# Attention projections of one decoder layer: the small matmul blocks between the weight chunks are gathered into one block per chunk

## The chip, the cores and the metric

One core of a Trainium2 chip runs the whole program. The metric is the device time of one execution in microseconds (us); for the kernel before it is the median of three runs. A profile of one further execution gives the trace. Five engines work side by side: PE (TensorE, matrix products), DVE (VectorE), ACT (ScalarE), POOL (GpSimd) and SP (SyncE, which here only issues transfers). PE reads SBUF and writes PSUM banks, which ACT and DVE empty.

## The reference, cut to what matters

One decoder layer is applied to 512 prompt rows and to 64 sample rows (8 sequences of 8 positions), with shared weights in float32:

```python
mod = silu(c) @ w_ada + b_ada          # 9 rows (1 prompt, 8 sample) x 6144, split in six
h = rmsnorm(x) * (1 + scale) + shift   # 512 + 64 rows of 1024
z = h @ w_in                           # q, k, v of three head groups, then u, v, gates
A = dilated attention per group        # group 0: window 128; 1: stride 4; 2: stride 16
B = spatial gating of u and v
x = x + gate1 * ((sig(gA) * A @ w_pa + sig(gB) * B @ w_pb) @ w_o)
x = x + gate2 * two-level mixture of experts(norm(x))
y = rmsnorm(x) modulated by silu(c) @ w_ada_final + b_ada_final
```

The keys and values of the sample rows' past come from three caches.

## The kernel before

**Weights come through a ring.** SP loads a list of pieces (`stream`, filled by `put`, `put_chunks` and `put_ada`) into four slots of 2 MB, in the list's order; piece n goes to slot n % 4 once piece n - 4 has been read (`wait_slot_read`). A weight chunk is 1024 x 512, loaded as two halves of 1 MB (k = 0 to 3 and 4 to 7). A half fills the front of its slot raw; ACT writes its rounded high part behind it (`split_to`, L1575), and DVE overwrites the raw values with the low part, raw minus high (L1891). The products of the 512 prompt rows use high and low parts in three passes: `three_passes`, L997 to L999, per tile of 128 rows and half 4 x 3 matmuls of 512 columns; `half_product` does one such tile.

**Sample rows.** Their product with a chunk is made from the raw values (`samples_product`, L1039: 16 matmul records of 256 columns for a half, in two 64-column parts of the array). So DVE may write the low part of a half only after PE has read its raw values: it waits in `wait_samples_read`.

**Modulation steps.** The rows `mod` that are needed later (G = 1 to 3, 2048 columns each) are computed between the attention projections, in eight steps k of one PSUM bank each (`ada_step`, L1012: 8 matmul records of 512 columns, in four 32-column parts of the array). A step needs 1 MB of weights, which is one piece of the ring, in a slot of its own.

**Order on PE.** For g = 0, 1, 2 there are three chunks q, k and w (w holds the v values). `project` runs half 0 on four tiles, then half 1 on four tiles. Inside a half, before tile `at_[half]`, it puts the sample product of one half: in half 0 that of the chunk's own second half, in half 1 that of the next chunk's first half. After each half comes one modulation step:

```python
                    if ada_from is not None:
                        ada_step(g + 1, ada_from + half)
```

So a k chunk has four small blocks: sample rows, step, sample rows, step. After w come transposes of q and k (L985), scores (L1174), exponentials on ACT (L1660), and values (`tile_values`, transposes at L985 and L1196), with steps 6 and 7 between the scores. For g < 2 the chunk q of the next group is computed before the values of the fourth tile; its first sample half comes before the values of the third. The ring's order is that of use: half, step, half, step for each chunk, then steps 6 and 7; after group 2 come the cached keys and values (SP issues from L726). `store_rows` sends finished modulation rows to DRAM, issued by SP five pieces behind a group's last step.

DVE empties k (L2077), ACT empties q and w (L1564); the list of PSUM users fixes the order.

Of the kernel before, what the change touches and what calls it, by code (L numbers as in the profile page):

```python
# [14 lines left out]
P = 128  # L15
D = 1024
KD = D // P
# [204 lines left out]
def build(nc, t, out):  # L222

    ctx = ExitStack()
    with ctx:
# [48 lines left out]
        def slot(n):  # L274
            return at((n % SLOTS) * SLOT, SLOT)
# [268 lines left out]
        ADA_COLS = 4 * CH  # L544
# [8 lines left out]
        def put(name, last, *srcs):  # L553
            S0.setdefault(name, []).extend(range(len(stream), len(stream) + len(srcs)))
            stream.extend(srcs)
            slot_last.extend(last)
            split.extend([False] * len(srcs))

        def put_chunks(name, last, w, js, between=None):

            for j, pair_ in zip(js, last):
                for m, h in zip(pair_, halves(w, j)):
                    put(name, [m], h)
                    split[-1] = True
                    if between is not None:
                        put_ada(between, 1)

        def paired(name, j):

# [20 lines left out]

            return [(mm.bank(m)[64 * q:64 * q + NS, 256 * q:256 * q + 256], slice(256 * q, 256 * q + 256)) for q in range(2)]

        def put_ada(G, count):
            w, _, col = ada[G]
            for _ in range(count):
                k = len(S0.get(f"ada{G}", []))
                put(f"ada{G}", [("ada", KD * G + k)],
                    w[k * P:(k + 1) * P, col * ADA_COLS:(col + 1) * ADA_COLS].unsqueeze(1))

        put_ada(0, KD)  # L600
        put_chunks("v", projected("v", 2), w_in, [QKV // CH + 2 + j for j in range(2)])
# [3 lines left out]
        for g in range(3):  # L605
            for j, x in enumerate("qkw"):
                put_chunks(f"{x}{g}", projected(f"{x}{g}"), w_in, [3 * j + g], between=g + 1)
            put_ada(g + 1, 2)
        caches = [t[f"cache_kv_w{w}"][0] for w in WINS]

        def keys_of(b, kv, g):
# [362 lines left out]
        def _(pe):  # L974
# [28 lines left out]

            def ada_step(G, k):

                n = S0[f"ada{G}"][k]
                slot_wait(n)
                if k == 0 and G:
                    pe.wait_ge(ada_out, G)
                w = slot(n)[:, 0:ADA_COLS].rearrange("p (j n) -> p j n", j=4)  # L1010
                for j in range(4):
                    ins = nc.tensor.matmul(ada_bank[32 * j:32 * j + 32, :], cT[:, k, :], w[:, j, :],  # L1012
                                           start=(k == 0), stop=(k == KD - 1))
                ins.then_inc(ada_read, 1)

            def project(name, lhs, j, g=0, ada_from=None, ahead=(None, None), at_=(1, 1), between=None):

                for half in range(2):
                    tiles = range(4) if paired(name, j) else range(TILES)
                    for i in tiles:  # L1020
                        if i == at_[half] and ahead[half] is not None:
                            samples_product(*ahead[half], 1 - half)
                        half_product(name, lhs, j, g, half, i)
                        if between is not None:
                            between(half, i)
                    if ada_from is not None:
                        ada_step(g + 1, ada_from + half)

            def samples_product(name, j, lhs, half):

# [166 lines left out]
                                               vn[:, kt, h * DH:(h + 1) * DH], start=(kk == 0), stop=(kk == nk - 1))  # L1197
                ins.then_inc(mm_filled, 1)

            def ahead_of(x, y):  # L1200

                return ((x, 0, h4_raw), (y, 0, h4_raw) if y else None)

            project("q0", H_PARTS, 0, ada_from=0, ahead=ahead_of("q0", "k0"), at_=(3, 3))
            for g in range(3):
                project(f"k{g}", H_PARTS, 0, g=g, ada_from=2, ahead=ahead_of(f"k{g}", f"w{g}"), at_=(3, 3))
                project(f"w{g}", H_PARTS, 0, g=g, ada_from=4, ahead=ahead_of(f"w{g}", None), at_=(3, 3))
                for j, src in enumerate((qn, kn)):

                    mm.wait_emptied(pe, mm.first[f"{'qk'[j]}{g}"] + TILES - 1)  # L1210
                    for i in range(TILES):
                        transposes(tp.first[f"qk{g}"], TILES * j + i, ROWS[i],
                                   [src[0:ROWS[i], i, k * P:(k + 1) * P] for k in range(4)])
                tp.wait_emptied(pe, tp.first[f"qk{g}"] + 2 * TILES - 1)
                tiles = GT[4 * g:4 * g + 4]
                tile_scores(*tiles[0])
                tile_scores(*tiles[1])
                ada_step(g + 1, 6)
                ada_step(g + 1, 7)
                tile_scores(*tiles[2])  # L1220
                tile_values(*tiles[0])
                tile_scores(*tiles[3])
                tile_values(*tiles[1])
                if g < 2:
                    samples_product(f"q{g + 1}", 0, h4_raw, 0)
                tile_values(*tiles[2])
                if g < 2:
                    project(f"q{g + 1}", H_PARTS, 0, g=g + 1, ada_from=0, ahead=ahead_of(f"q{g + 1}", f"k{g + 1}"),
                            at_=(1, 3))
                tile_values(*tiles[3])  # L1230


            def key_tile(b, x):
# [638 lines left out]
        def _(dve):  # L1872
# [11 lines left out]
            def split_to(last):  # L1884

                for n in range(parted[0], min(last + 1, N_SLOTS)):
                    if split[n]:
                        raw, hi, lo = half_slot(n)
                        dve.wait_ge(hi_done, halves_to[n])
                        wait_samples_read(dve, n)  # L1890
                        V.tensor_tensor(lo, raw, hi, ALU.subtract).then_inc(lo_done, 1)  # L1891
                    parted[0] = n + 1
# [173 lines left out]
            for g in range(3):  # L2066
                split_to(S0[f"k{g}"][1])
                if g:
                    dve.wait_ge(kv_out, 16 * KV_OUTS[g - 1])
                for i in tile_order(f"k{g}", 0):  # L2070
                    n = ROWS[i]
                    m = bank_of(f"k{g}", 0, i)
                    if i == 3:
                        split_to(S0[f"w{g}"][0])
                    mm.wait_filled(dve, m)
                    for src, cols in quarters(m) if i == 4 else [(mm.bank(m), slice(0, CH))]:
                        ins = V.tensor_copy(kn[0:n, i, cols], src)  # L2077
                    ins.then_inc(mm_dve, 1)
                split_to(S0[f"w{g}"][1])
                dve.wait_ge(abias_in, 16 * (g + 2))  # L2080
                add_bias(*GT[4 * g])
                add_bias(*GT[4 * g + 1])
                ada_rows(g + 1)
                for i in (2, 3):
                    add_bias(*GT[4 * g + i])
                    copy_out(g, i - 2)
                if g < 2:
                    split_to(S0[f"q{g + 1}"][0])
                copy_out(g, 2)
                if g < 2:  # L2090
                    split_to(S0[f"k{g + 1}"][0])
                copy_out(g, 3)

            def group_differences():
# [412 lines left out]
```

## Time and profile before

| | |
|---|---|
| median of 3 runs | 1317.78 us (1312.26 to 1319.25) |
| the profiled execution | 1314.65 us |
| its span, first to last instruction | 1313.0 us |
| PE busy | 1237.6 us, 94% of the span |
| DVE, ACT, POOL busy | 50%, 42%, 15% |
| mean granted clock of PE | 0.982 of full speed |
| transfers | 293.96 MB, mean 224 GB/s |

The span is 1.65 us shorter than the time of that execution. The stretch in which the change lies runs from about 264 to 603 us of the span. Matmul durations overlap each other, so the cost of a block is read from the start of its first matmul to the start of what follows.

### The profile page before, as it was taken

Reading aid. Unit: us, or ns where it says so; the run is one execution under the profiler, and the core shown is the slowest. Engines: PE = TensorE matmul, PEld = TensorE weight load, DVE = VectorE, ACT = ScalarE, POOL = GpSimd, SP = SyncE. Lnnn points to the kernel's source line nnn. Section 1 sums busy time; section 2 is a strip of 40 time slices with the busy share of each in tenths; the row PEclk is TensorE's granted clock in tenths of the full one; section 3 lists DMA queues with packets and bytes.
Section 4 is the critical chain, followed back from the end, with each engine's and each line's share of the span. In section 5 each row is a group of like instructions: output and inputs, shape, how many; then the busy total and the mean of one; then the engine's idle time right before and its main releaser. Section 6 shows DMA issues by size and latency. Waiting matters only on the chain.

```text
span 1313.0 us, 17979 instructions
## 1 busy us (share of the span) xinstructions
PE 1237.6 (94%) x7160; PEld 941.9 (72%) x7160; DVE 661.7 (50%) x920; ACT 548.7 (42%) x878; POOL 194.0 (15%) x228
## 2 busy tenths in 40 slices
PE   4899999999999999999889999999989999999996
PEld 1677877776778887887756666747757887777762
DVE  1328513222161205032377551255687888888877
ACT  3623313002272126214433332211446787777852
POOL 1202200020000010001200010100034122222320
PEclk9899999999999999999799999999989999999999
DMA  9552221154443454537689995911399999999982
GB/s 357 209 209 76 94 64 64 65 190 173 152 146 85 159 178 176 171 128 275 238 295 382 384 374 172 304 64 53 104 318 296 371 374 374 372 373 378 366 301 91
DMA packets 126235, 293.96 MB, mean 224 GB/s; under 512 B 10160, under 2 KB 10288, under 8 KB 121496
## 3 DMA queue, kind: packets, MB, share of 16 engines
q1 hardware_dynamic: 108216, 243.57, 52.7%
q0 software_dynamic: 17952, 49.44, 10.5%
q8 instruction: 49, 0.80, 0.2%
q14 instruction: 18, 0.15, 0.0%
HBM read 269.91 MB, written 30.42 MB: 229 GB/s over the span
## 4 chain that ended last, share of the span: by engine, by line
PE 78%; DMA 11%; DVE 4%; ACT 4%; issue 2%; POOL 2%; SPq 0%; DVEq 0%; ACTq 0%; POOLq 0%
PE psum L997 18%; PE psum L999 17%; PE psum L998 17%; PE psum L985 5%; PE psum L1039 5%; DMA arena<-in_cache_kv_w_dram 3%; DMA arena<-in_w_gate_dram 2%; PE psum L1360 2%; PE psum L1196 2%; PE psum L1012 2%; DMA arena<-in_w_ada_dram 2%; PE psum L1268 2%; ACT arena L1564 1%; POOL slots_d L915 1%; PE psum L1174 1%
## 5 line engine op out<-in xcount | busy, mean ns | idle before, releaser
L997 PE MATMUL psum<-part,part 128*128 128x512 f32 (+1 forms) x1088 | 442.4, 407 | 10.6 <-DVE part L1942 5.0
L999 PE MATMUL psum<-part,part 128*128 128x512 f32 (+1 forms) x1088 | 429.4, 395 | 0.0
L998 PE MATMUL psum<-part,part 128*128 128x512 f32 (+1 forms) x1088 | 429.3, 395 | 0.0
L997 PEld LDWEIGHTS psum<-part,part 128*128 128x128 f32 (+1 forms) x1088 | 227.4, 209 | 74.3 <-issue 24.8
L999 PEld LDWEIGHTS psum<-part,part 128*128 128x128 f32 (+1 forms) x1088 | 227.3, 209 | 40.1
L998 PEld LDWEIGHTS psum<-part,part 128*128 128x128 f32 (+1 forms) x1088 | 228.1, 210 | 35.7
L2360 DVE TENSOR_TENSOR part<-arena,part 128x2048 fp32r<-128x2048 f32 x96 | 218.9, 2291 | 33.5 <-ACT part L1792 32.3
L1891 DVE TENSOR_TENSOR part<-arena,part 128x2048 fp32r<-128x2048 f32 x42 | 96.4, 2301 | 254.5 <-PE psum L1039 228.7
L1792 ACT ACTIVATE part<-arena 128x2048 fp32r<-128x2048 f32 x94 | 179.7, 1919 | 45.1 <-DMA arena<-in_w_down_dram 19.5
L1564 ACT ACTIVATE arena<-psum 128x512 f32<-128x512 f32 (+3 forms) x140 | 75.9, 567 | 248.4 <-PE psum L999 202.7
L1575 ACT ACTIVATE part<-arena 128x2048 fp32r<-128x2048 f32 x42 | 80.0, 1910 | 173.2 <-DMA arena<-in_w_in_dram 168.6
L985 PE MATMUL psum<-cst,arena 128*128 128x128 f32 (+2 forms) x858 | 117.7, 282 | 26.9 <-DMA cst<-in_consts_dram 12.4
L985 PEld LDWEIGHTS psum<-cst,arena 128*128 128x128 f32 (+2 forms) x858 | 96.2, 146 | 57.0 <-issue 15.9
L1039 PE MATMUL psum<-arena 128*64 128x256 f32 x544 | 66.0, 385 | 0.2 <-DMA arena<-in_w_in_dram 0.2
L169 ACT ACTIVATE arena<-psum 128x512 f32<-128x512 f32 x56 | 33.4, 596 | 57.7 <-PE psum L985 57.6
L2043 DVE TENSOR_TENSOR arena<-psum,arena 128x512 f32<-128x512 f32 x30 | 19.0, 684 | 75.1 <-PE psum L1174 66.4
L1039 PEld LDWEIGHTS psum<-arena 128*64 128x64 f32 x544 | 36.1, 136 | 25.6 <-issue 9.1
L950 POOL DMA_INDIRECT yd<-arena x15 | 32.4, 2161 | 98.3 <-issue 91.5
L1268 PE MATMUL psum<-arena 128*32 128x136 f32 (+1 forms) x832 | 37.8, 284 | 9.1 <-ACT arena L169 5.9
L171 DVE COPY arena<-psum 128x512 f32<-128x512 f32 x48 | 33.0, 687 | 21.6 <-PE psum L985 21.2
L1660 ACT ACTIVATE arena<-arena 128x128 f32<-128x128 f32 (+1 forms) x96 | 39.6, 419 | 6.9 <-DVE arena L2049 6.9
L1012 PE MATMUL psum<-arena 128*32 128x512 f32 x256 | 35.8, 642 | 6.3 <-DMA arena<-in_w_ada_dram 6.3
(289 smaller groups left out, 1071.2 us busy)
## 6 DMA issues: line engine op xcount, KB each, us to landing
arena<-in_w_in_dram SPq DMA_DIRECT2D x34, 1024.0 KB, 5.5
arena<-in_cache_kv_w_dram SPq DMA_DIRECT2D x16, 2048.0 KB, 11.9
arena<-in_w_gate_dram SPq DMA_DIRECT2D x32, 1024.0 KB, 9.9
arena<-in_w_up_dram SPq DMA_DIRECT2D x32, 1024.0 KB, 9.4
arena<-in_w_down_dram SPq DMA_DIRECT2D x32, 1024.0 KB, 10.2
arena<-in_w_ada_dram SPq DMA_DIRECT2D x24, 1024.0 KB, 7.7
arena<-in_cache_kv_w_dram SPq DMA_DIRECT2D x16, 1024.0 KB, 9.0
arena<-in_w_ada_final_dram SPq DMA_DIRECT2D x8, 1024.0 KB, 7.9
```

What stands on the lines that cost most here:

```text
L985: ins = nc.tensor.transpose(bank[0:a.shape[-1], k * n:k * n + a.shape[0]], a, c_("ident", a.shape[0])[:, 0:a.shape[0]])
L997: nc.tensor.matmul(out_, hi, w_hi, start=start, stop=False)
L998: nc.tensor.matmul(out_, hi, w_lo, start=False, stop=False)
L999: last_product[0] = nc.tensor.matmul(out_, lo, w_hi, start=False, stop=stop)
L1012: ins = nc.tensor.matmul(ada_bank[32 * j:32 * j + 32, :], cT[:, k, :], w[:, j, :], start=(k == 0), stop=(k == KD - 1))
L1039: ins = nc.tensor.matmul(out_, lhs[:, 4 * half + k, :], raw[:, k, cols], start=(half == 0 and k == 0), stop=(half == 1 and k == 3))
L1268: ins = nc.tensor.matmul(mm.bank(m)[r, cols], Qm[:, b % 2 * 2048 + quad * 512 + j * P:b % 2 * 2048 + quad * 512 + (j + 1) * P][:, r], KT[: ...
L1564: nc.scalar.activation(dst, ring.bank(m)[0:n, 0:cols] if src is None else src, func, scale=scale).then_inc(ring.done(m), 1)
L1575: nc.scalar.activation(hi, raw, ACT.Copy).then_inc(hi_done, 1)
L1792: nc.scalar.activation(hi, raw, ACT.Copy).then_inc(e_hi, 1)
L1891: V.tensor_tensor(lo, raw, hi, ALU.subtract).then_inc(lo_done, 1)
L2360: V.tensor_tensor(lo, raw, hi, ALU.subtract).then_inc(e_lo, 1)
```

## The change

The two modulation steps that followed the two halves of a chunk become one piece of the ring: 256 rows x 2048 columns, 2 MB, the two rows of a partition side by side in one slot. Steps 6 and 7 also share a piece. `ada_at` says where a step is found. The 42 pieces of the three groups become 30.

On PE, `project` of a k or w chunk has nothing between its tiles. A new `between_chunks` runs between chunks: both sample halves of the next chunk, then two modulation steps. After w there are the two steps alone. The q chunks keep the sample product of their own second half inside half 0 (before the second tile; for q0 it was before the fourth). For q1 and q2 the block that prepares k stands behind the values of the fourth tile. DVE makes the low part of k's first half after it has copied out those values, where it was before.

```diff
@@ -562,8 +562,8 @@
                     put(name, [m], h)
                     split[-1] = True
-                    if between is not None:
-                        put_ada(between, 1)
+                if between is not None:
+                    put_ada(between, 2, 2)
...
-        def put_ada(G, count):
+        ada_at = [[] for _ in ada]
+
+        def put_ada(G, count, together=1):
+
             w, _, col = ada[G]
-            for _ in range(count):
-                k = len(S0.get(f"ada{G}", []))
-                put(f"ada{G}", [("ada", KD * G + k)],
-                    w[k * P:(k + 1) * P, col * ADA_COLS:(col + 1) * ADA_COLS].unsqueeze(1))
+            for _ in range(count // together):
+                k = len(ada_at[G])
+                rows = w[k * P:(k + together) * P, col * ADA_COLS:(col + 1) * ADA_COLS]
+                ada_at[G] += [(len(stream), c) for c in range(together)]
+                put(f"ada{G}", [("ada", KD * G + k + together - 1)], rows.rearrange("(k p) n -> p k n", p=P))
...
-            put_ada(g + 1, 2)
+            put_ada(g + 1, 2, 2)
...
-                    if ada_from is not None:
-                        ada_step(g + 1, ada_from + half)
+
+            def between_chunks(following, G, k):
+
+                if following is not None:
+                    for half in range(2):
+                        samples_product(following, 0, h4_raw, half)
+                for step in range(2):
+                    ada_step(G, k + step)
...
-            project("q0", H_PARTS, 0, ada_from=0, ahead=ahead_of("q0", "k0"), at_=(3, 3))
+            project("q0", H_PARTS, 0, ahead=(("q0", 0, h4_raw), None))
+            between_chunks("k0", 1, 0)
             for g in range(3):
-                project(f"k{g}", H_PARTS, 0, g=g, ada_from=2, ahead=ahead_of(f"k{g}", f"w{g}"), at_=(3, 3))
-                project(f"w{g}", H_PARTS, 0, g=g, ada_from=4, ahead=ahead_of(f"w{g}", None), at_=(3, 3))
+                project(f"k{g}", H_PARTS, 0, g=g)
+                between_chunks(f"w{g}", g + 1, 2)
+                project(f"w{g}", H_PARTS, 0, g=g)
+                between_chunks(None, g + 1, 4)
...
-                    project(f"q{g + 1}", H_PARTS, 0, g=g + 1, ada_from=0, ahead=ahead_of(f"q{g + 1}", f"k{g + 1}"),
-                            at_=(1, 3))
+                    project(f"q{g + 1}", H_PARTS, 0, g=g + 1, ahead=((f"q{g + 1}", 0, h4_raw), None))
                 tile_values(*tiles[3])
+                if g < 2:
+                    between_chunks(f"k{g + 1}", g + 2, 0)
...
                 if g < 2:
-                    split_to(S0[f"k{g + 1}"][0])
+                    split_to(S0[f"q{g + 1}"][1])
                 copy_out(g, 3)
```

## Rows read from the trace of the kernel before

**Rows 1.** The page: PE's share of the chain that ended last.
```profile
PE 78%; DMA 11%; DVE 4%; ACT 4%; issue 2%; POOL 2%; SPq 0%; DVEq 0%; ACTq 0%; POOLq 0%
```

**Rows 2.** Busy time by stretch: PE, PEld, DVE, ACT, POOL, clock, DMA share, GB/s.
```profile
283.00:365.00 82.00, 80.32 (x422) 56.81 (x421) 14.99 (x11) 18.91 (x27) 2.15 (x4) 1.00 0.47 167
...
645.00:825.00 180.00, 168.54 (x1728) 118.92 (x1727) 99.23 (x299) 65.08 (x188) 22.05 (x38) 0.98 0.92 324
```

**Rows 3.** Lines L1039 and L1012 on PE, 274 to 645 us: records, nanoseconds.
```profile
L1039 PE MATMUL psum<-arena x272: 379/379/431, 283.1 to 587.2; 128*64 128x256 f32 x136
...
L1012 PE MATMUL psum<-arena x192: 592/593/617, 287.9 to 615.2; 128*32 128x512 f32 x192
```

**Rows 4.** Timeline of PE: a sample block between two products of group 0.
```profile
297.01 0.39 PE L999 MATMUL psum<-part,part 128*128 128x512 f32 x1
297.32 1.95 PE L1039 MATMUL psum<-arena 128*64 128x256 f32 x16
299.20 0.50 PE L997 MATMUL psum<-part,part 128*128 128x512 f32 x1
299.54 0.40 PE L998 MATMUL psum<-part,part 128*128 128x512 f32 x1
```

**Rows 5.** Timeline of PE in q1: a modulation step between two products.
```profile
407.43 0.39 PE L998 MATMUL psum<-part,part 128*128 128x512 f32 x1
407.66 0.40 PE L999 MATMUL psum<-part,part 128*128 128x512 f32 x1
407.99 1.06 PE L1012 MATMUL psum<-arena 128*32 128x512 f32 x8
408.99 0.62 PE L997 MATMUL psum<-part,part 128*128 128x512 f32 x1
409.45 0.40 PE L998 MATMUL psum<-part,part 128*128 128x512 f32 x1
```

**Rows 6.** Timeline of PE: two sample halves, and two steps, without a gap.
```profile
819.85 3.67 PE L1039 MATMUL psum<-arena 128*64 128x256 f32 x32
823.45 1.06 PE L1314 MATMUL psum<-cst,arena 128*128 128x8 f32 x8
...
368.85 1.92 PE L1012 MATMUL psum<-arena 128*32 128x512 f32 x16
370.70 2.82 PE L1174 MATMUL psum<-arena 64*128 64x128 f32 x32
```

**Rows 7.** Timeline of PE: 32-column work, then a sample block.
```profile
784.14 2.78 PE L1306 MATMUL psum<-arena 128*32 128x512 f32 x24
786.85 1.95 PE L1039 MATMUL psum<-arena 128*64 128x256 f32 x16
```

**Rows 8.** Timeline of PE at the end of q1.
```profile
422.79 1.06 PE L1012 MATMUL psum<-arena 128*32 128x512 f32 x8
423.79 1.09 PE L985 MATMUL psum<-cst,arena 128*128 128x128 f32 x8
```

**Rows 9.** Timeline of ACT at the end of q1.
```profile
422.90 0.60 ACT L1564 ACTIVATE arena<-psum 128x512 f32<-128x512 f32 x1 [2.65 <-PE psum L999]
```

**Rows 10.** Timeline of PE, and the chain: the sample block that w0's load holds up.
```profile
325.42 0.39 PE L999 MATMUL psum<-part,part 128*128 128x512 f32 x1
326.00 1.95 PE L1039 MATMUL psum<-arena 128*64 128x256 f32 x16 [0.19 <-DMA arena<-in_w_in_dram]
...
320.40 5.55 DMA arena<-in_w_in_dram
```

**Rows 11.** Timeline of DVE: the low part of k0's first half.
```profile
299.39 2.29 DVE L1891 TENSOR_TENSOR part<-arena,part 128x2048 fp32r<-128x2048 f32 x1 [11.91 <-PE psum L1039]
```

**Rows 12.** Transfers issued at L726, 590 to 700 us: PE's waits for them.
```profile
  PEld psum L985: 0.4, 1
  PE psum L985: 0.2, 1
```

**Rows 13.** Busy time at the end of group 2, columns as in rows 2.
```profile
626.00:641.00 15.00, 13.33 (x63) 12.41 (x63) 3.58 (x6) 8.36 (x35) 2.16 (x4) 0.54 0.43 159
```

**Rows 14.** Timeline of PE in that stretch.
```profile
628.13 1.97 PE L985 MATMUL psum<-cst,arena 128*128 128x128 f32 x8 [1.49 <-ACT arena L1660]
```

More of the change, by code:

```diff
@@ L1004, in ada_step @@
             def ada_step(G, k):
-                n = S0[f"ada{G}"][k]
+                n, c = ada_at[G][k]
                 slot_wait(n)
@@ L1009, in ada_step @@
                     pe.wait_ge(ada_out, G)
-                w = slot(n)[:, 0:ADA_COLS].rearrange("p (j n) -> p j n", j=4)
+                w = slot(n)[:, c * ADA_COLS:(c + 1) * ADA_COLS].rearrange("p (j n) -> p j n", j=4)
                 for j in range(4):
@@ L1014, in ada_step, with project @@
                 ins.then_inc(ada_read, 1)
-            def project(name, lhs, j, g=0, ada_from=None, ahead=(None, None), at_=(1, 1), between=None):
+            def project(name, lhs, j, g=0, ahead=(None, None), at_=(1, 1), between=None):
                 for half in range(2):
@@ L1198, in tile_values @@
                 ins.then_inc(mm_filled, 1)
-            def ahead_of(x, y):
-                return ((x, 0, h4_raw), (y, 0, h4_raw) if y else None)
-            project("q0", H_PARTS, 0, ada_from=0, ahead=ahead_of("q0", "k0"), at_=(3, 3))
+            project("q0", H_PARTS, 0, ahead=(("q0", 0, h4_raw), None), at_=(3, 3))
+            between_chunks("k0", 1, 0)
             for g in range(3):
-                project(f"k{g}", H_PARTS, 0, g=g, ada_from=2, ahead=ahead_of(f"k{g}", f"w{g}"), at_=(3, 3))
-                project(f"w{g}", H_PARTS, 0, g=g, ada_from=4, ahead=ahead_of(f"w{g}", None), at_=(3, 3))
+                project(f"k{g}", H_PARTS, 0, g=g)
+                between_chunks(f"w{g}", g + 1, 2)
+                project(f"w{g}", H_PARTS, 0, g=g)
+                between_chunks(None, g + 1, 4)
                 for j, src in enumerate((qn, kn)):
```

## The prediction

> **What bounds the kernel now.** I read the page first, for the chain that ended last: PE carries 78% of it [rows 1]. So time taken out of PE's own sequence counts, if what follows is not bound by something else. Next the busy time by stretch. In the attention projections PE is busy 80.3 of 82 us at full clock with transfers at 0.47 of their capacity; in the stage of the cached keys that follows, transfers are at 0.92 [rows 2]. The change lies in the first kind of stretch, and what it saves must pass through the second. Third, the lines: 272 records of sample products are 17 blocks of 16, and 192 of modulation steps are 24 steps of 8, all between 283 and 616 us [rows 3]. The change keeps every one of them; it alters only what stands beside them. So I went to the timeline of PE and measured edges, from start to start.
>
> **What an edge costs.** A modulation step in q1: products start 0.23 us apart, the step starts 0.33 us after the last product, it occupies 1.00 us until the next product starts, and the second product comes 0.46 us behind the first, where the pace is 0.23 [rows 5]. The edge in and out is 0.10 + 0.22 = 0.32 us. In group 0, where the prompt rows are contiguous and not taken with stride 4, the same two gaps are 0.31 and 0.34, so 0.08 + 0.11, about 0.20 us for both, and the sample half occupies 1.88 us [rows 4]. Two sample halves that follow each other take 3.60 us until the next work starts, not 3.76, and two steps take 1.85 us, not 2.00 [rows 6]. So each block ends with about 0.15 us in which the array empties, and a neighbour of the same kind saves that.
>
> **Group 0.** Between products there were ten blocks: q0's own second half, step, k0's first half, step; in k0 four; in w0 two. One more step stands at the end of w0. Now there are three (q0's sample half, and one block before k0 and one before w0). Seven edges less are 7 x 0.20 = 1.40 us. Five pairs of equals have come together (sample with sample twice, step with step three times, the end of w0 included): 5 x 0.155 = 0.78 us. Sum 2.2 us.
>
> **A wait that goes.** The sample product for w0 starts 0.58 us after the product before it, where others take 0.31: w0's first half, issued at 320.40, took 5.55 us to land [rows 10]. It was waiting for the slot of k0's first half, two tiles before use. In the new order it takes the slot of the modulation piece read before k0, a whole chunk ahead. 0.26 us off, once; the other such blocks don't wait.
>
> **Groups 1 and 2.** Nine blocks stood between products (q three, k four, w two); two remain (q's own second half, the block before w). 7 x 0.32 = 2.24 us. The five pairs give 0.78 again. The step at the end of q goes from there: it took 1.00 us up to the transposes [rows 8], and is counted in a pair. The block that takes it in stands behind the values instead, where products began anyway with their slow first gap. For this new boundary I charge one emptying, 0.15 us, bounded by 0 and by the 0.32 of a full edge. Sum 2.87 us for each group, 5.7 for both.
>
> **Inside the new block** there is one meeting of unlike kinds: 64-column sample products, then 32-column steps. No row shows that order. The reverse order does: 24 matmuls of 32 columns take 2.71 us until the sample block starts [rows 7], which is 24 x 0.107 (half of a step's pace of 0.85 for 8, from rows 6) plus 0.15, a full emptying. I take it as not saved. If it were free, six blocks would give 6 x 0.15 = 0.9 us more. The Trainium skill, "TensorEngine Tiling (Array Packing)", section Key Properties, says that changing the tiling mode, not just the tile, drains TensorE; by it the meeting costs the emptying, as I took it. The rows at hand agree, with the 0.15 us of rows 7, but it also appears where like follows like with another output.
>
> **What could be late now.** (a) The low part of k's first half. DVE started it 2.07 us after the sample block's start and needs 2.29 us [rows 11]; that block began at 297.32 [rows 4]: ready after 4.4 us. The first product comes 3.60 + 1.85 = 5.45 us after the block's start: 1.1 us of slack, covered by the second sample half and the steps. DVE's copy of the values, now ahead of it, ends before the raw half is read. Without that cover each of six blocks would lose up to 4.4 us less what still stood in between. (b) The second half of the next chunk must be in when its raw product starts. Its slot is free after the first tile of the running chunk's second half. From rows 10, the issue would be at 320.40; three tiles of 12 products at 0.23 (2.75 us each), the edge and one sample half of 1.7 us put its use some 10.0 us later. The load took 5.55 us there: 4.4 us of slack. (c) The 2 MB modulation piece is issued when a chunk ends and used a chunk (22 us) later. SP's other issues are not moved past anything that PE needs: the row stores still stand five pieces behind the last step, behind a piece that waits for the same chunk q, and the pieces number 12 fewer, a multiple of four, so every later piece keeps its slot. (d) ACT: at the end of q1 it emptied the last tile from 422.90 to 423.50, under cover of the step [rows 9]. With the transposes 1.0 us earlier, their first tile would be ready at about 423.4, so ACT is late by 0.1 us at most, twice. DVE now copies k's last tile after w's low part, 5 us into the block; its bank is asked for three tiles into w. Nothing.
>
> **Sum.** 2.2 + 0.3 + 5.7 - 0.1 = 8.1 us, with bounds of 7.4 (the new boundary at 0.32, ACT late by 0.2 each time) and 9.3 (both free). The profiled execution took 1314.65 us, 3.1 under the median of 1317.78; from it the change gives 1306.5, from the median 1309.7. The three runs and the profiled one average 1316.0. I say 1308. What a measurement of this kernel can tell from no change is 0.5%, 6.6 us; 8.1 us is 0.62%, just over.
>
> **Rivals.**
> (1) The saving is partly absorbed. The key stage runs on transfers at 0.92. If the transfers were already the limit when group 2 ends, PE would only wait longer. For: the share. Against: PE's waits for these transfers from 590 to 700 us are 0.4 and 0.2 us [rows 12], and the cached pieces are issued as the ring's slots come free, which moves with PE. Gains in group 2 alone (2.9 us) would be at risk first, then all. I put it at a gain of 2 to 5 us: 1311 to 1315. Chance 0.13.
> (2) The clock. At the end of group 2 PE waits 1.49 us for exponentials and then works at about half clock: eight transposes take 1.97 us, not 1.09 [rows 8, 14], granted clock 0.54 over 15 us [rows 13]. That costs up to 13.3 x 0.46 = 6.1 us. The same waits come 8 us earlier. If the fall comes at another point of that sequence, the gain may grow to 12 us or shrink to 3. The rows can't say which. Also, longer unbroken runs of products change nothing where the clock is already 1.00 [rows 2]. 1303 to 1306 with chance 0.08, 1311 to 1314 with 0.09.
> (3) Slower: the second half lands late. Place: all six new blocks, where PE stands at the raw product with everything behind it. The price is the landing time less 10.0 us. It would eat the whole gain at 8.1 / 6 = 1.35 us each, so at landings of 11.4 us; slower by 0.5% at 2.45 us each, landings of 12.5 us, which gives 1325. Transfers do take that long in crowded stretches. Against: 5.55 us in just this place [rows 10] and a DMA share of 0.47, and nothing else is queued ahead on SP. Chance 0.07.
> (4) The edges shrink the forecast: the emptying belongs to what follows and is paid once per block whatever precedes, so only edges go and the pairs give nothing: 1.4 + 2 x 2.1 + 0.3 = 5.9 us, 1310 from my base, within 0.5%. Against it, rows 6. Chance 0.06.
> The forecast itself: 0.57.
>
> **How the numbers follow.** Faster by over 0.5%: of the forecast's 0.57 I count 0.50 (7.4 to 9.3 us is over 6.6, and some of it is lost to the measurement's spread), the clock's good side 0.08, and 0.04 of the rest: 0.62. Slower by over 0.5%: rival 3 and little else, 0.08. Within: 0.30. The range: the forecast's own, 1305 to 1311, is widened by the runs' spread of 7 us (1312.26 to 1319.25) to about 1302 to 1314. It takes in the good side of the clock at the low end and the absorbed gain up to the old median at the high end: 1301 to 1317. What is left out is the late landing and the far tails.
>
> **What the profile after would show.** Two runs of 96 products without a break in k and w of each group; before them 32 records of L1039 and 16 of L1012 that take 5.4 to 5.5 us to the next product. The steps 6 and 7 of the first group should end about 2.5 us earlier than at 370.7 [rows 6], and the last matmul of a step should start about 8 us earlier than at 615.2 [rows 3]. Waits of PE for DVE's low part or for w_in near zero. From 660 us on, everything earlier by one constant. Wrong would be: a first product that waits for DVE behind a block (a), a gap in the middle of L1039's 32 records (b), or an interval from the last step to the first key scores that has grown (rival 1 or 2).

## The result, and the profile after

The new kernel takes 1311.21 us (median of 19 runs, 1306.88 to 1317.64) against 1319.25 us (19 runs, 1312.26 to 1323.95): ratio 0.9944, 95% interval 0.9928 to 0.9961. The ratio makes it 7.4 us less, 5.1 to 9.5 by the interval; the two medians are 8.0 apart. The forecast was 8.1 us, and a time of 1308.

One thing was misread ahead of the prediction. The new line for q0 is `project("q0", H_PARTS, 0, ahead=(("q0", 0, h4_raw), None), at_=(3, 3))`: q0's sample block stays before the fourth tile, as in the kernel before, and is not moved to the second. No term of the sum used it.

**The blocks on PE.** The new line numbers are 4 to 10 higher: L1001 to L1003 are the three passes, L1049 the sample products, L1016 the modulation steps, L989 the transposes. The timeline of PE in the profiled execution of the new kernel, at the boundary from q0 to k0, at the end of q1, and at the start of k1:

```profile
298.15 0.39 PE L1003 MATMUL psum<-part,part 128*128 128x512 f32 x1
298.47 3.67 PE L1049 MATMUL psum<-arena 128*64 128x256 f32 x32
302.07 1.92 PE L1016 MATMUL psum<-arena 128*32 128x512 f32 x16
303.93 0.50 PE L1001 MATMUL psum<-part,part 128*128 128x512 f32 x1
304.26 0.39 PE L1002 MATMUL psum<-part,part 128*128 128x512 f32 x1
...
416.03 0.40 PE L1003 MATMUL psum<-part,part 128*128 128x512 f32 x1
416.27 0.49 PE L989 MATMUL psum<-cst,arena 128*128 128x128 f32 x3
...
422.72 3.67 PE L1049 MATMUL psum<-arena 128*64 128x256 f32 x32
426.33 1.92 PE L1016 MATMUL psum<-arena 128*32 128x512 f32 x16
428.18 0.63 PE L1001 MATMUL psum<-part,part 128*128 128x512 f32 x1
```

From start to start: 3.60 us for two sample halves, 1.86 for two steps, and the same edges as in [rows 4]. The meeting of the sample products with the steps saves nothing: the samples take 3.60 us to the next start here, as before other work in [rows 6]. The end of q1 holds what the prediction missed: transposes right behind products start 0.24 us after the last one, at the pace of the products. The step that stood there before started 0.33 us behind them, an entry edge of 0.10 that is gone as well.

A sample half that products on 64 columns follow, in the gate chunk of the new kernel:

```profile
185.57 1.95 PE L1049 MATMUL psum<-arena 128*64 128x256 f32 x16
187.45 0.44 PE L1001 MATMUL psum<-part,part 128*64 128x512 f32 x1
```

It takes 1.88 us up to them, as it does up to products on the full array.

**The waits.** All waits of PE between 262 and 600 us of the new kernel (line, who released it; sum, times, longest):

```profile
PE psum L989 <- ACT arena L1574: 3.1, 13, 0.3
PE psum L1206 <- ACT arena L1574: 2.6, 8, 0.4
PE psum L1184 <- ACT arena L1574: 0.9, 2, 0.5
PE psum L989 <- ACT arena L1670: 0.8, 1, 0.8
```

None is for DVE's low part, none for a transfer. The wait of [rows 10] is gone. DVE still starts 2.06 us after the block, and the loads of the chunk halves land as fast as before; first the timeline of DVE, then the time from issue to landing of the 16 issues of w_in between 262 and 600 us:

```profile
300.53 4.50 DVE L1901 TENSOR_TENSOR part<-arena,part 128x2048 fp32r<-128x2048 f32 x2 [13.41 <-PE psum L1049]
```

```profile
DMA to landing us min/median/max: 5.2/5.4/7.8
```

The longest, 7.8 us, is below the 10.0 that the second half has.

**Where the gain stands along the way.** I count from the start of the sample block near 264 us, a block that both kernels have just ahead of the change, to the first transpose behind w2. In the kernel before 264.50 to 604.26, so 339.76 us; in the new one 264.15 to 595.50, so 331.35 us: 8.41 us less. Group by group it is 2.56, 2.93 and 2.92.

Behind that point the sequence is that of the kernel before. The busy time of the stretch that answers to [rows 13], in the new kernel (PE, PEld, DVE, ACT, POOL, clock, DMA share, GB/s):

```profile
617.00:632.00 15.00, 13.33 (x64) 12.41 (x64) 3.47 (x5) 8.46 (x36) 2.05 (x4) 0.58 0.15 52
645.00:825.00 180.00, 166.94 (x1625) 117.01 (x1626) 95.92 (x290) 62.04 (x180) 21.05 (x37) 0.98 0.91 323
```

The clock falls at the same work, with the same 1.49 us of wait in front of it. The span of the profiled execution is only 4.8 us shorter as a whole (1308.2 against 1313.0). PE's share of the chain that ended last went from 78% [rows 1] to 73%; the page of the new kernel:

```profile
span 1308.2 us, 17967 instructions
...
PE 73%; DMA 14%; ACT 4%; DVE 4%; issue 3%; POOL 2%; SPq 0%; DVEq 0%; ACTq 0%; POOLq 0%
```

The chain now passes through more transfers of w_gate in the experts (5% of the span, before 2%), some 500 us behind the change. Whether that belongs to the change is a question for the experiments.

### The profile page after: what moved, and what is told of

Same layout as the page of the kernel before. It is cut to its first block, busy times and chain, and to the rows that moved or that the text cites. A ratio compares the mean times of both kernels' runs of the same rounds, so it can differ in the third digit from the quotient of the medians.

```text
span 1308.2 us, 17967 instructions
## 1 busy us (share of the span) xinstructions
PE 1231.0 (94%) x7160; PEld 941.8 (72%) x7160; DVE 660.4 (50%) x920; ACT 547.9 (42%) x878; POOL 194.9 (15%) x228
## 4 chain that ended last, share of the span: by engine, by line
PE 73%; DMA 14%; ACT 4%; DVE 4%; issue 3%; POOL 2%; SPq 0%; DVEq 0%; ACTq 0%; POOLq 0%
PE psum L1001 17%; PE psum L1003 16%; PE psum L1002 16%; DMA arena<-in_w_gate_dram 5%; PE psum L989 5%; PE psum L1049 5%; DMA arena<-in_cache_kv_w_dram 3%; PE psum L1370 2%; PE psum L1206 2%; PE psum L1016 2%; ACT arena L1574 2%; DMA arena<-in_w_ada_dram 2%; DMA arena<-in_w_in_dram 1%; PE psum L1278 1%; POOL slots_d L919 1%
## 5 line engine op out<-in xcount | busy, mean ns | idle before, releaser
L1001 PE MATMUL psum<-part,part 128*128 128x512 f32 (+1 forms) x1088 | 439.0, 404 | 11.4 <-DVE part L1952 5.9
L1003 PE MATMUL psum<-part,part 128*128 128x512 f32 (+1 forms) x1088 | 429.6, 395 | 0.0
L1001 PEld LDWEIGHTS psum<-part,part 128*128 128x128 f32 (+1 forms) x1088 | 227.6, 209 | 66.2 <-issue 13.4
L1003 PEld LDWEIGHTS psum<-part,part 128*128 128x128 f32 (+1 forms) x1088 | 227.5, 209 | 40.1
L989 PE MATMUL psum<-cst,arena 128*128 128x128 f32 (+2 forms) x858 | 117.0, 281 | 25.8 <-DMA cst<-in_consts_dram 11.7
L989 PEld LDWEIGHTS psum<-cst,arena 128*128 128x128 f32 (+2 forms) x858 | 95.2, 145 | 55.4 <-issue 17.6
L1049 PE MATMUL psum<-arena 128*64 128x256 f32 x544 | 64.7, 384 | 0.2 <-DMA arena<-in_w_in_dram 0.2
L1049 PEld LDWEIGHTS psum<-arena 128*64 128x64 f32 x544 | 36.6, 136 | 24.5 <-issue 8.2
L1278 PEld LDWEIGHTS psum<-arena 128*32 128x32 f32 (+1 forms) x832 | 29.3, 117 | 15.9 <-issue 13.5
```

The costliest lines, as they stand in the source:

```text
L989: ins = nc.tensor.transpose(bank[0:a.shape[-1], k * n:k * n + a.shape[0]], a, c_("ident", a.shape[0])[:, 0:a.shape[0]])
L1001: nc.tensor.matmul(out_, hi, w_hi, start=start, stop=False)
L1003: last_product[0] = nc.tensor.matmul(out_, lo, w_hi, start=False, stop=stop)
L1049: ins = nc.tensor.matmul(out_, lhs[:, 4 * half + k, :], raw[:, k, cols], start=(half == 0 and k == 0), stop=(half == 1 and k == 3))
L1278: ins = nc.tensor.matmul(mm.bank(m)[r, cols], Qm[:, b % 2 * 2048 + quad * 512 + j * P:b % 2 * 2048 + quad * 512 + (j + 1) * P][:, r], KT[: ...
```

## The experiments

The theory to test: the gain is PE time at the edges of small blocks, plus the emptying that neighbours of one kind share; the pairing of the pieces only makes the gathering possible; the order inside the block hides DVE. The rivals: larger transfers help by themselves; the order inside doesn't matter; a part of the gain is lost to the transfers of the later stages.

Times stand as ratios to the kernel before, with intervals. The distance is that from the sample block near 264 us to the first transpose after w2, read from the starts on PE.

| kernel | distance, us | against the new one | ratio |
|---|---|---|---|
| before, three profiles | 339.76, 339.92, 340.09 | +8.4 to +8.7 | 1 |
| new, four profiles | 331.35, 331.37, 331.35, 331.35 | 0 | 0.9944, again 0.9941 |
| old order, paired pieces | 339.54 | +8.19 | 1.0 (0.9981 to 1.0019) |
| new order, single pieces | 367.69 | +36.3 | 1.0165 (1.0126 to 1.0203) |
| only the steps gathered | 338.18 | +6.83 | 0.9983 (0.9962 to 1.0004) |
| only the samples gathered | 333.97 | +2.62 | 0.9947 (0.9928 to 0.9965) |
| steps first in the block | 336.21 | +4.86 | 0.997 (0.9954 to 0.9986) |
| carried further | 331.01 | -0.34 | 0.993 (0.9912 to 0.9948) |

The distance repeats to 0.02 us over four profiles of the new kernel and to 0.33 over three of the kernel before, so it tells apart what times of 1300 us with a spread of 10 can't. The other kernels have one profile each.

### The pieces alone, with the old order

```diff
-            between_chunks("k0", 1, 0)
+            project("q0", H_PARTS, 0, ada_from=0, ahead=ahead_of("q0", "k0"), at_=(3, 3))
...
+                    if ada_from is not None and half in step_after:
+                        ada_step(g + 1, ada_from + step_after.index(half))
```

> PE does its blocks in the order of the kernel before; only the ring's pieces are those of the new kernel (two steps in one 2 MB piece, 30 pieces and not 42). Theory (the gain is the edges beside the small blocks): nothing but the wait for w0's first half goes, 0.3 us; the transposes after w2 start within 0.5 us of the kernel before, reckoned from the first sample block at 264 us, and the ratio to it is 1.000. Rival (fewer and larger transfers are what helps): several us faster, ratio near 0.995.

The distance is 0.22 us shorter than in the first profile of the kernel before and 0.55 shorter than in the third, the wait of [rows 10] and little more, and the ratio is 1.0. PE waits for no transfer of w_in in this stretch. Fewer and larger transfers bring nothing by themselves.

### The new order, each step in a piece of its own

```diff
-                    put_ada(between, 2, 2)
+                    put_ada(between, 2)
...
-            put_ada(g + 1, 2, 2)
+            put_ada(g + 1, 2)
```

> PE does its blocks in the order of the new kernel, but each modulation step keeps a piece and a slot of its own. Theory (the pairing's work is to free a slot, so that the next chunk's second half is in when its sample product is gathered): that half now waits for the slot of the running chunk's second half, so it is issued at the chunk's end and lands 5.5 us later, 3.9 us too late, before k0 and before w0, w1 and w2; before k1 and k2 the values cover most of it. Some 16 us of waits of PE for w_in, time about 1326, ratio to the kernel before about 1.006. Rival (pieces don't matter, only the order on PE): the same as the new kernel, ratio 0.994.

The time is 1342.09 us (4 runs), 16 us more than the theory gave. The timeline of PE between q0 and k0, then busy time and clock there and in k0:

```profile
298.58 1.95 PE L1049 MATMUL psum<-arena 128*64 128x256 f32 x16
303.95 3.68 PE L1049 MATMUL psum<-arena 128*64 128x256 f32 x16 [3.42 <-DMA arena<-in_w_in_dram]
307.56 2.83 PE L1016 MATMUL psum<-arena 128*32 128x512 f32 x16
310.32 0.50 PE L1001 MATMUL psum<-part,part 128*128 128x512 f32 x1
```

```profile
298.00:312.00 14.00, 10.58 (x58) 4.95 (x58) 5.34 (x4) 3.00 (x4) 0.00 (x0) 0.76 0.32 99
312.00:332.00 20.00, 20.00 (x89) 16.52 (x88) 2.07 (x3) 1.92 (x1) 0.00 (x0) 1.00 0.38 141
```

The wait itself is as forecast: 3.42 us here, 16.7 us over five blocks, where the theory had about 16.

```profile
PE psum L1049 <- DMA arena<-in_w_in_dram: 16.7, 5, 3.6
```

What it left out is what comes behind a wait. The second sample half took 3.61 us and not 1.88, the steps 2.76 and not 1.85, at a granted clock of 0.76 over the stretch; in k0 the clock is back at 1.00. In the five blocks together the work behind the waits took 10.1 us more than at full clock. 0.75 us more are the halves that are no longer joined. Of the 36.3 us that leaves 8.8, and 7.6 of them lie in one place, the attention of group 1, which takes 35.0 us and not 27.4 up to the first product of q2. The timelines of ACT and PE there, then PE's busy time and clock behind the wait:

```profile
510.87 1.91 ACT L1585 ACTIVATE part<-arena 128x2048 fp32r<-128x2048 f32 x1 [3.78 <-DMA arena<-in_w_in_dram]
515.91 0.77 PE L989 MATMUL psum<-cst,arena 128*128 128x128 f32 x5 [2.45 <-ACT arena L1670]
```

```profile
515.90:535.30 19.40, 18.71 (x105) 0.65 0.27 110
```

ACT splits the first half of q2 before it makes the exponentials, and that half landed late. So PE waits 2.45 us for the exponentials, where it waits 0.84 in the new kernel, and the clock behind that wait is 0.65. The price of the rival "the second half lands late" has two parts. Directly at the blocks, 16.7 us of waits cost about 27; with the late exponentials the whole is about double the waits. The point at which it would have turned the gain into a loss was nearer than the prediction put it.

### One kind of block gathered, the other left spread

Only the steps:

```diff
-            between_chunks("k0", 1, 0)
+            between_chunks(None, 1, 0)
...
-                project(f"k{g}", H_PARTS, 0, g=g)
-                between_chunks(f"w{g}", g + 1, 2)
+                project(f"k{g}", H_PARTS, 0, g=g, ahead=ahead_of(f"k{g}", f"w{g}"), at_=(3, 3))
+                between_chunks(None, g + 1, 2)
```

> From the new kernel, with the sample products back inside the chunks (the next chunk's first half before the last tile, a chunk's own second half before its last tile of half 0); the two steps stay together between chunks. Theory: six places get two edges more and lose one shared emptying: two in group 0 at 2 x 0.20 + 0.15, four at 2 x 0.32 + 0.15, so 4.3 us later than the new kernel when the transposes after w2 start. Rival (only the number of blocks in a chunk boundary matters for DVE's low part, not edges): no change at that point.

It came out at 6.83 us, 2.5 more than forecast. PE's waits in this kernel from 262 to 604 us have a line that neither the kernel before nor the new one has, and the timeline shows the place, k1 (it repeats at k2):

```profile
PE psum L1001 <- DVE part L1905: 2.3, 2, 1.1
```

```profile
426.73 1.92 PE L1016 MATMUL psum<-arena 128*32 128x512 f32 x16
429.78 0.62 PE L1001 MATMUL psum<-part,part 128*128 128x512 f32 x1 [1.13 <-DVE part L1905]
```

```profile
426.83 0.69 DVE L2069 COPY arena<-psum 128x512 f32<-128x512 f32 x1 [26.25 <-PE psum L1206]
427.44 2.28 DVE L1905 TENSOR_TENSOR part<-arena,part 128x2048 fp32r<-128x2048 f32 x1
```

DVE copies out the values first and makes the low part after that, an order that this kernel kept from the new one. Only the steps stand in front of the product now, 1.85 us, and DVE needs 3.0. The edges and lost joinings account for 4.3 (the forecast's sum), the two waits for 2.3: 6.6 of 6.83. So the reordering in DVE's program, costed at nothing, is free only because the sample halves stand in the block too.

Only the samples:

```diff
-                for step in range(2):
+                for step in range(2 if following is None else 1):
                     ada_step(G, k + step)
...
+                    if half == 0 and step is not None:
+                        ada_step(*step)
```

> From the new kernel, with the second step of each pair moved out of the block to behind half 0 of the next chunk; both sample halves stay together. Theory: six places get one edge more and lose one shared emptying: two at 0.20 + 0.15, four at 0.32 + 0.15, so 2.6 us later than the new kernel when the transposes after w2 start, and no wait for the low part, as one step and the second sample half still cover 4.6 us of the 4.4 needed. If that cover is too thin, up to 0.3 us more in each of six places.

2.62 us, as forecast, and no wait for DVE. One step behind the samples is cover enough. This is the plainest test of the edges: six places at one edge and one emptying each.

### The block turned round

```diff
+                for step in range(2):
+                    ada_step(G, k + step)
                 if following is not None:
                     for half in range(2):
                         samples_product(following, 0, h4_raw, half)
-                for step in range(2):
-                    ada_step(G, k + step)
```

> From the new kernel, with the block turned round: the two steps first, then the two sample halves. The same edges and the same work. Theory (the steps behind the samples cover DVE's low part of the next chunk's first half): that part is ready 4.36 us after the first sample product starts, and the products now come after 3.6 us, so each of six blocks makes PE wait about 0.8 us: 4.8 us later when the transposes after w2 start, with DVE L1901 named as what ended the waits. Rival (DVE has slack anyway): no change.

4.86 us, as forecast, and all of it where PE waits for DVE. From the start of the samples to the first product it is 4.41 us in each of the six blocks, the 4.4 that the prediction said DVE needs, and not 3.60: six times 0.81. The profile counts a wait from the modelled end of the matmul before it, so its own sum is smaller:

```profile
PE psum L1001 <- DVE part L1901: 4.4, 6, 0.7
```

```profile
304.91 0.50 PE L1001 MATMUL psum<-part,part 128*128 128x512 f32 x1 [0.74 <-DVE part L1901]
```

The same matmuls and the same edges, and over half of the gain on PE is lost.

### A pad behind the last projection

```diff
+                        if g == 2 and j == 0 and i == 0:
+                            tp.wait_empty(pe, tp.first["qk2"])
+                            for k in range(60):
+                                nc.tensor.transpose(tp.bank(tp.first["qk2"])[:, 0:P], src[:, 0, 0:P], c_("ident"))
```

> From the new kernel, with 60 transposes of one tile repeated ahead of the transposes after w2, whose result is overwritten: about 8 us more for PE (60 at 0.136) at the end of the last projection. Theory (what is saved on PE there passes to the end): everything after is 8 us later and the time returns to that of the kernel before, ratio 1.000 within 0.002. Rival (the key stage and the experts run at the rate of the transfers and take up such a shift): the time stays near that of the new kernel, ratio 0.994 to 0.997.

The pad took 6.60 us, not 8 (60 transposes without a gap run at 0.11 us each; I had taken their pace from blocks with waits). Reckoned from the sample block near 264 us, the key stage's first gathering of heads, L1314 before and its like here, comes 4.9 to 6.3 us later than in the four profiles of the new kernel. The time is 1314.78 us, against 1310.41 for the new kernel on the same chip: 4.4 us more, ratio 0.9976 (0.9959 to 0.9993) against 0.9941 (0.9922 to 0.9959). The ratio lies between the theory's 1.000 and the rival's 0.994 to 0.997, and its interval reaches both. By the medians 4.4 of 6.6 us, most of the shift, pass to the end. With intervals this wide, a loss of 1 to 2 us in the later stages is neither shown nor excluded. The profile holds a chance loss of its own. PE waits 2.13 us for the cached keys, the granted clock is 0.50 behind that (774 to 776 us), and the key stage takes 138.0 us, where the new kernel takes 134.5 or 134.6 in three of four profiles:

```profile
772.74 1.74 PE L989 MATMUL psum<-cst,arena 128*128 128x128 f32 x8 [2.13 <-DMA arena<-in_cache_kv_w_dram]
```

### The new kernel and the kernel before once more

> The new kernel unchanged, for a second profile and for times on the same chip as the others. From both theories: the transposes after w2 again start 8.4 us earlier than in the kernel before (reckoned from the first sample block), ratio 0.9944. What it tells is how much the stages after 825 us differ between two executions of one kernel: if by 1 to 3 us, the 2.9 us that the first profile gave back there are such a difference and not part of the change.

> The kernel before unchanged, for a second profile. Question: PE's wait for w_in in front of the second sample half of the first gate chunk of the last stage (ga0, near 790 us). Theory (the key stage ends on its transfers, and a PE that arrives earlier waits there): no wait in this kernel, as in its first profile. Rival (that wait comes by chance in either kernel): a wait of 1 to 3 us in at least one of two further profiles of this kernel.

> The kernel before unchanged, for a third profile; the same question and the same expectations as for the second.

> The new kernel unchanged, for a third profile. Theory (PE arrives earlier and meets the transfers): a wait for w_in of 0.2 to 3 us before ga0's second sample half, near 782 us; where it is over 2 us the granted clock falls behind it and the stage takes 3 to 5 us longer. Rival (chance): no wait in at least one of the two further profiles.

> The new kernel unchanged, for a fourth profile; the same question and the same expectations as for the third.

The second profile of the new kernel stood 4.7 us behind its first at the end, with an equal distance up to w2. The place was a wait before the second sample half of ga0. Its timeline, and busy time and clock from there:

```profile
783.12 3.68 PE L1049 MATMUL psum<-arena 128*64 128x256 f32 x16 [2.13 <-DMA arena<-in_w_in_dram]
786.73 0.80 PE L1001 MATMUL psum<-part,part 128*128 128x512 f32 x1
```

```profile
783.00:786.70 3.70, 3.58 (x16) 1.72 (x16) 0.00 (x0) 3.19 (x2) 0.00 (x0) 0.50 1.04 338
```

In the first profile of the new kernel the same wait was 0.23 us and the block took 1.88:

```profile
782.05 1.95 PE L1049 MATMUL psum<-arena 128*64 128x256 f32 x16 [0.23 <-DMA arena<-in_w_in_dram]
```

I took this for the absorption of rival 1: PE arrives earlier and meets the transfers. The four further profiles say otherwise. The kernel before waits there too, 0.2 us in its second profile and 0.8 in its third, and none in its first; the new kernel doesn't wait at all in its third and fourth. So the wait comes and goes in both. Where it was 2.13 us the clock fell and the key stage took 139.3 us and not 134.5 (between the first and last gathering of heads; three profiles before: 134.2, 134.9, 134.8; four of the new one: 134.5, 139.3, 134.5, 134.6). It was 2.7 and 2.3 us, with the clock falling, in the kernels with only the samples gathered and with the idea carried further, and it was never over 1 us in the profiles of the kernel before or of the other experiments. That makes it somewhat likelier for a kernel that arrives early, but with these counts I don't call it shown. The kernel before met neither of its two expectations: its waits of 0.2 and 0.8 us are not none, and not over 1.

The part from the products with w_pa to the last combination of the experts' rows varies by up to 5.6 us in one kernel, which is not far from the gain: 429.6, 432.6, 430.2 us in the kernel before, 432.2, 433.2, 427.9, 433.5 in the new one. So the 2.6 us that the first pair of profiles lost there, with its transfers of w_gate in the chain, is within the spread of one kernel.

Up to the key stage the seven profiles show no loss. From the sample block near 264 us to the first gathering of heads it is 425.6, 427.4 and 426.4 us in the kernel before and 417.9, 417.8, 417.3 and 418.8 in the new one: 8.5 us less on the average. The prediction named a grown interval from the last step to the first key scores as the sign of rival 1 or 2. It has not grown: from the last matmul of a step to L1268 and its like it is 28.5, 28.5 and 28.2 us before, and 28.4, 28.5, 27.6 and 28.5 in the new kernel.

### The idea carried further

```diff
-            project("gb", H_PARTS, 0, ahead=(None, ("gb", 1, h4_raw)), at_=(4, 4))
+            project("gb", H_PARTS, 0)
+            for half in range(2):
+                samples_product("gb", 1, h4_raw, half)
...
-                    project(f"q{g + 1}", H_PARTS, 0, g=g + 1, ahead=((f"q{g + 1}", 0, h4_raw), None))
+                    samples_product(f"q{g + 1}", 0, h4_raw, 1)
+                    project(f"q{g + 1}", H_PARTS, 0, g=g + 1)
```

> From the new kernel, the same idea carried to three more places: the second sample halves of q1 and q2 stand directly before the chunk, behind the values, not inside it, and both sample halves of the second gate chunk stand between its predecessor and the transposes. Theory: 2 x 0.2 us and 0.55 us less, about 1 us in all, ratio to the kernel before 0.9935; too little to tell from the new kernel by time, so read by the starts on PE. Rival (the low parts come too late in these places): PE waits for DVE there and the microsecond is lost.

On PE, q1 and q2 give the 0.34 us of the table, where 0.4 was expected. The gate chunks give 1.16 (from the mixing products at 151.6 us to the first sample block of `pb`, 62.40 us in the new kernel and 61.24 here), twice the forecast: two edges and a joining, and a wait for emptied banks that the block now covers. The timeline of PE in this kernel:

```profile
187.89 0.39 PE L1003 MATMUL psum<-part,part 128*64 128x512 f32 x1
188.21 3.67 PE L1049 MATMUL psum<-arena 128*64 128x256 f32 x32
191.81 0.71 PE L989 MATMUL psum<-cst,arena 64*128 64x64 f32 x8
```

1.5 us less in all. The time is 1309.78 us (6 runs), ratio 0.993 (0.9912 to 0.9948) against 0.9941 (0.9922 to 0.9959) for the new kernel on the same chip. It beats the kernel before; that it beats the new one is shown on PE's timeline alone.

## Why the prediction was right, step by step

- **Edges and emptyings.** Right. Forecast were 2.2 us in group 0 and 0.26 for the wait, 2.56 measured; 2.87 in groups 1 and 2, 2.93 and 2.92 measured. The small rests have several parts. The prediction let the entry edge of 0.10 us at the end of q stand. The five pairs are worth 0.72 us and not 0.78, since two single steps take 1.99 us and two joined ones 1.85. In group 0 an edge is 0.22 us and not 0.20: the products just behind a block also come a little slower than the 0.227 us of a long run. The new boundary before k cost what was charged: 0.12 us up to the block, and 0.03 in the first product behind it (0.47 to the second one, against 0.44 behind the values before). The two kernels with one kind gathered give the same prices from the other side: six edges and six emptyings at 2.62 (forecast 2.6), and twelve edges and six emptyings at 4.5 (forecast 4.3) when the waits for DVE are taken off.
- **The meeting of unlike kinds** costs a full emptying, as taken from the reverse order in [rows 7]. That is also what the Trainium skill says of changed tiling modes ("TensorEngine Tiling (Array Packing)", section Key Properties). The trace agrees in both orders: two halves take 3.60 us up to the steps, and with the block turned round two steps take 1.85 us up to the samples. It does not show that the change of mode is the cause. The sample half of the gate chunk shown above is followed by products that use 64 columns too, and its 1.88 us are the same as in front of products on the full array. The 0.9 us kept in the upper bound did not exist.
- **Cover.** (a) Right: 4.4 us are needed, 5.45 are there. With 3.6 in place of it the products come 0.81 us later per block; with 1.85 and DVE's copy ahead PE waits 1.1. (b) Right: landings of 5.2 to 7.8 us against 10.0. (c), (d) Right: no wait appeared, and PE's wait for ACT grew by 0.05 us at the end of q1 (0.25 to 0.30) and of q2 (0.34 to 0.39).
- **The order of DVE's program** was costed at nothing, rightly for this block. The reason given (the copy ends before the raw half is read) holds only with the sample halves in the block.
- **From PE to the end.** 8.4 us on PE became 7.4 by the runs (5.1 to 9.5). Nothing lost is shown, and up to the key stage nothing is lost. Rival 1 (absorption) has one possible place, ga0's second half, where the wait of 2.13 us cost the new kernel's second profile 4.6 us; it also occurs, shorter, in the kernel before. The pad of 6.6 us came out at 4.4 in time. That the time came so close to the forecast is in part luck: the interval of the measured gain is over 4 us wide, and the forecast of 1308 lies 3 under the median, since it was taken from a base of 1316 and the 19 runs of the kernel before give 1319.
- **The clock** (rival 2) didn't move in the way feared: the fall at the end of group 2 came at the same work in both kernels.
- **The late landing** (rival 3) was unlikely for the reason given, but its price was set too low: in the kernel with single pieces 16.7 us of wait came with 36.3 us lost, 7.6 of them at one later place.
- **Rival 4** (joined pairs give nothing) is refuted by the timeline: 3.60 and 1.86 us for two, where singles take 1.88 and 1.00 each.

## What to carry to other kernels

Between long runs of products, count blocks, not matmuls: every small block of another kind costs its edge (0.22 to 0.32 us here) and an emptying (about 0.15 us), and neighbours of the same kind share the latter. Gathering needs the operands of a whole block at once, so look first at which ring slot they must wait for, and then put last in the block what covers the engine that prepares the next product. Read such small gains by the distance between two starts on PE, which repeated to 0.02 us in the new kernel and to 0.33 in the one before, and not by the time of the whole, which spread by 10.

## What was not expected of the hardware

- Waits of a few us were followed by the lower of the two clock levels (1.2 GHz in place of 2.4): after 3.42 us of waiting the next 16 sample matmuls took 3.61 us and not 1.88, at a granted clock of 0.76 over 14 us, and after 2.13 us the granted clock was 0.50 for 3.7 us. After waits of 0.2 to 1.1 us between products it stayed at 1.00. The length of the wait alone does not tell: in the key stage of the kernel before, the clock stayed at 1.00 with a longest wait of 1.8 us, while at the end of group 2 it fell with one of 1.49 [rows 13, 14].
- Transposes behind products start at the pace of the products (0.24 us), while the blocks that use 64 or 32 columns of the array at a time start 0.32 to 0.33 us behind them.
- The stage of the experts, 430 us long, differs by up to 5.6 us between executions of one kernel.
